# One hybrid decoder step on one core: expert programs written out instead of looped, the sample's dots read from PSUM, and 16 dots placed later

## The reference, cut to what matters

```python
def peer_ffn(h, wq, subkeys, u_tab, v_tab):            # h: normalised x, 1024 wide
    q = (xb @ wq).reshape(.., 8 heads, 2, 128)
    s = jnp.einsum('thpd,pkd->thpk', q, subkeys)        # two sets of 128 keys
    s1, i1 = lax.top_k(s[:, :, 0], 16); s2, i2 = lax.top_k(s[:, :, 1], 16)
    cand = s1[..., :, None] + s2[..., None, :]
    top_s, sel = lax.top_k(cand, 16)                    # 16 experts per head, of 16384
    g = jax.nn.softmax(top_s, axis=-1)
    u = u_tab[idx]
    act = jax.nn.gelu(jnp.einsum('thkd,td->thk', u, xb))
    vv = v_tab[idx]
    return jnp.einsum('thk,thkd->td', g * act, vv)
```

## Time and profile before

| | |
|---|---|
| runs of the kernel before | 2018.54, 2015.97, 2029.83 us (median 2018.54) |
| the profiled execution | 2016.57 us |
| its span | 2014.8 us |
| mean granted clock of TensorE, share of full speed | 0.903 |
| busy, share of the span | PE 78%, DVE 60%, POOL 56%, ACT 24% |
| DMA over the span | 713.45 MB, mean 354 GB/s |
| sample's mixer ends (last dot of tile 0) | 694.2 us |
| tiles 1 and 2 in the loops | about 960 to 1640 us |
| tile 3, straight | about 1640 to 1930 us |

### The profile page before, as it was taken

One profiled execution on the slowest core, in us unless ns is written; L12 is line 12 of the kernel. 1 busy time (PEld: TensorE's weight loads), 2 busy tenths in 40 slices (PEclk: granted clock), 3 DMA queues, 4 the chain that ended last, 5 costly groups with the idle time before them and its releaser, 6 DMA issues.

```text
span 2014.8 us, 20816 instructions
## 1 busy us (share of the span) xinstructions
PE 1579.8 (78%) x5461; PEld 746.2 (37%) x5461; DVE 1208.6 (60%) x3129; ACT 473.8 (24%) x1217; POOL 1122.4 (56%) x1168
## 2 busy tenths in 40 slices
PE   6989989987459358768788888698879789799943
PEld 1534546552127013214333344243334334354410
DVE  2223265869767602116667766667776579879973
ACT  1131313121001122212322222223232223332321
POOL 3000020223863545777777667667777767777774
PEclk9989999998775689998999989899999899999966
DMA  9796577798994799999999999999999999999997
GB/s 324 242 362 219 203 257 255 254 376 193 375 382 148 255 412 390 406 413 370 410 420 419 400 368 414 416 342 420 419 402 391 391 378 419 406 419 417 418 367 290
DMA packets 237576, 713.45 MB, mean 354 GB/s; under 512 B 23101, under 2 KB 49055, under 8 KB 237456
## 3 DMA queue, kind: packets, MB, share of 16 engines
q0 software_dynamic: 156672, 570.49, 72.4%
q1 hardware_dynamic: 80488, 140.73, 19.7%
q10 hardware_dynamic: 312, 1.07, 0.2%
HBM read 704.42 MB, written 8.25 MB: 354 GB/s over the span
## 4 chain that ended last, share of the span: by engine, by line
PE 18%; DMA 17%; DVE 10%; POOL 8%; issue 8%; ACT 3%; DVEq 0%; POOLq 0%; ACTq 0%
PE ps_y L2357 12%; DMA v_rows<-in_peer_v_dram,expert_idx_ring 7%; DMA v_rows<-in_peer_v_dram,tile_idx 6%; DVE u_rows L2136 5%; DMA u_rows<-in_peer_u_dram,expert_idx_ring 4%; PE ps_r L2331 4%; POOL u_rows L1916 3%; POOL v_rows L1922 3%; PE ps_y L2385 2%; POOL v_rows L1930 2%; ACT wt_diag L2027 1%; DVE key_scores_w L2147 1%; DVE top_i L2149 0%; DVE top L2148 0%; DVE top_i L2150 0%
## 5 line engine op out<-in xcount | busy, mean ns | idle before, releaser
L2357 PE MATMUL ps_y<-v_rows,wt_diag 128*128 128x512 f32 x1536 | 736.0, 620 | 140.3 <-DMA v_rows<-in_peer_v_dram,expert_idx_ring 75.1
L2357 PEld LDWEIGHTS ps_y<-v_rows,wt_diag 128*128 128x128 f32 x1536 | 285.7, 197 | 529.5 <-issue 515.6
L2136 DVE CUSTOM_DVE_ANT_0 u_rows<-u_rows,ps_y 128x1024 f32<-128x1024 f32 x360 | 420.6, 1217 | 70.5 <-DMA u_rows<-in_peer_u_dram,expert_idx_ring 64.4
L1916 POOL DMA_INDIRECT u_rows<-in_peer_u_dram,expert_idx_ring x384 | 369.6, 963 | 155.3 <-issue 92.3
L1922 POOL DMA_INDIRECT v_rows<-in_peer_v_dram,expert_idx_ring x384 | 365.2, 951 | 123.0 <-issue 99.6
L341 POOL DMA_INDIRECT low_rows<-in_peer_u_dram,tile_idx x128 | 165.6, 1294 | 210.3 <-DVE tile_dots L333 123.2
L608 PE MATMUL ps_z<-w_stream,hT 128*128 128x512 f32 (+5 forms) x560 | 245.9, 596 | 25.9 <-DVE hT L784 15.5
L2385 PE MATMUL ps_y<-v_rows,wt_diag 64*64 64x512 f32 x1024 | 134.7, 643 | 57.9 <-DMA v_rows<-in_peer_v_dram,tile_idx 53.7
L333 DVE CUSTOM_DVE_ANT_0 low_rows<-low_rows,tile_rows 128x1024 f32<-128x1024 f32 x128 | 153.2, 1230 | 40.6 <-DMA low_rows<-in_peer_u_dram,tile_idx 40.0
L1930 POOL DMA_INDIRECT v_rows<-in_peer_v_dram,tile_idx x128 | 121.4, 948 | 72.9 <-PE ps_y L2385 45.6
L608 PEld LDWEIGHTS ps_z<-w_stream,hT 128*128 128x128 f32 (+1 forms) x560 | 99.9, 183 | 150.5 <-issue 119.6
(11 more groups left out here) (442 smaller groups left out, 1691.7 us busy)
## 6 DMA issues: line engine op xcount, KB each, us to landing
w_stream<-in_w_in_dram SPq DMA_DIRECT2D x25, 2048.0 KB, 11.6
w_stream<-in_ada_w_dram SPq DMA_DIRECT2D x12, 2048.0 KB, 12.9
w_stream<-in_peer_wq_dram SPq DMA_DIRECT2D x8, 1024.0 KB, 8.3
wq<-in_peer_wq_dram SPq DMA_DIRECT2D x4, 2048.0 KB, 42.4
w_stream<-in_w_in_dram SPq DMA_DIRECT2D x5, 1568.0 KB, 9.6
w_stream<-in_w_in_dram SPq DMA_DIRECT2D x5, 1536.0 KB, 11.0
u_rows<-in_peer_u_dram,expert_idx_ring POOLq DMA_INDIRECT x384, 8.9
v_rows<-in_peer_v_dram,expert_idx_ring POOLq DMA_INDIRECT x384, 9.0
```

Source lines behind the costliest of these rows:

```text
L1916: g.indirect_dma_start(u_rows[:, j, :], None, U, bass.IndirectOffsetOnAxis(where[:, j:j + 1], 0))\
L2136: v.tensor_tensor_reduce(u_rows[:, j, :], u_rows[:, j, :], row[:, :], 1.0, 0.0, ALU.mult, ALU.add, dots[:, par, j:j + 1]).then_inc(s["u_us ...
L2357: mm = nc.tensor.matmul(ps_y[:, c * 512:(c + 1) * 512], diag[:, par, j, :], v_rows[:, j, c * 512:(c + 1) * 512], start=(first and j == 0), ...
```

## The change

1. The loops over t on POOL, ACT, DVE and PE, and the inner loops over pairs on ACT and PE, become Python loops: the programs of tiles 1 and 2 are written out, with constants for every wait and address.
2. A new method `row_to` copies `h0`, the dots' row, into two PSUM banks on DVE, and from there on the dots read it in PSUM. It is called three times: into `ps_n` in front of gap (3, "Z"), into `ps_z` in front of gap L, and into `ps_n` again in front of gap O. For this, OZ is copied out by ACT early (`act_oz`, right behind `act_front`), DVE waits for that before gap L and for `int_ready` before gap O, and PE waits for the dots up to gap L before it writes the attention scores into `ps_n`, and for the dots up to gap O before the output product goes into `ps_z`.
3. `DOTS_IN` has 3 dots instead of 6, 7 and 6 in the three gaps in front of the gates, and 16 more in gaps C to N. The gathers move with them.
4. Two semaphores of the constants become one; the waits stay where they were.

```diff
-           (3, "B"): 2, (3, "C"): 3, (3, "D"): 2, (3, "E"): 4, (3, "F"): 3, (3, "G"): 3, (3, "I"): 2, (3, "R"): 4, (3, "Z"): 6,
-           ("sample", "A"): 7, ("sample", "B"): 6, ("sample", "C"): 5, ("sample", "D"): 3, ("sample", "E"): 8,
-           ("sample", "F"): 5, ("sample", "G"): 5, ("sample", "K"): 6, ("sample", "L"): 9, ("sample", "N"): 12,
+           (3, "B"): 2, (3, "C"): 3, (3, "D"): 2, (3, "E"): 4, (3, "F"): 3, (3, "G"): 3, (3, "I"): 2, (3, "R"): 4, (3, "Z"): 3,
+           ("sample", "C"): 8, ("sample", "D"): 6, ("sample", "E"): 10, ("sample", "F"): 6, ("sample", "G"): 7,
+           ("sample", "K"): 8, ("sample", "L"): 11, ("sample", "N"): 13, ("sample", "O"): 12, ("sample", "Z"): 11}
...
-            self.nc.vector.tensor_tensor_reduce(self.rows[:, k % NB, :], self.rows[:, k % NB, :], self.X.h0[:, :], 1.0, 0.0,
+            self.nc.vector.tensor_tensor_reduce(self.rows[:, k % NB, :], self.rows[:, k % NB, :], self.row, 1.0, 0.0,
                                                 ALU.mult, ALU.add, self.keep["dots0"][:, k:k + 1]).then_inc(self.s["a_used"], 1)
+
+    def row_to(self, chain, banks):
+
+        self.row = banks[:, :, :].rearrange("p a n -> p (a n)")
+        chain(self.nc.vector.tensor_copy(self.row, self.X.h0[:, :]))
...
-        T.pool_og(pool)
+        T.pool_og(pool, oz_copied=True)
...
         T.act_front(act, chain)
+        T.act_oz(act)
...
         def behind_rows(eng):
 
+            eng.wait_ge(before["piece_out"], len(PIECES))
+            X.ahead.row_to(chain, X.ps_n01)
             left(eng)
             T.gap(eng, "A")
...
+        T.z_out(dve, OZ)
+        X.ahead.row_to(chain, X.ps_z01)
         T.gap(dve, "L")
...
+        dve.wait_ge(s["int_ready"], 1)
+        X.ahead.row_to(chain, X.ps_n01)
         T.gap(dve, "O")
...
         T.t_out(pe, S_K1)
+        pe.wait_ge(before["a_used"], DOTS_AT[("sample", "L")])
...
+        pe.wait_ge(before["a_used"], DOTS_AT[("sample", "O")])
         T.out_product(pe, lambda eng: T.on(eng, "oa_ready"), lambda eng: T.t_out(eng, S_HM))
...
-                with pool.Fori(0, LT - 1) as t:
+                for t in range(0, LT - 1):
                     for p in range(2, PPT + 2):
...
-                with act.Fori(0, LT - 1) as t:
-                    with act.Fori(1, PPT - 3) as p:
+                for t in range(0, LT - 1):
+                    for p in range(1, PPT - 3):
...
-                with dve.Fori(0, LT - 1) as t:
+                for t in range(0, LT - 1):
...
-                with pe.Fori(0, LT - 1) as t:
-                    with pe.Fori(1, PPT - 2) as p:
+                for t in range(0, LT - 1):
+                    for p in range(1, PPT - 2):
```

More of the change, by code:

```diff
@@ L114, in __init__ @@
         self.ident_ready, self.cleared, self.dist_ready = sem("const_ident"), sem("const_cleared"), sem("const_dist")
-        self.sdist_ready, self.s_step = sem("const_sdist"), sem("const_s_step")
+        self.s_step = sem("const_s_step")
         self.pool_ready = sem("const_pool")
@@ L129, in constants_dve @@
         v.memset(C.cols[h * NS:(h + 1) * NS, 1:2], -SLOPES[h])
-    dve.wait_ge(C.sdist_ready, 1)
+    dve.wait_ge(C.dist_ready, 1)
     v.tensor_tensor(C.tpat[:, :], C.tpat[:, :], K["ident"][:, :], ALU.mult).then_inc(C.s_step, 1)
@@ L139, in constants_dve @@
         .then_inc(C.s_step, 1)
-    dve.wait_ge(C.dist_ready, 1)
+    dve.wait_ge(C.dist_ready, 2)
     for h in range(AH):
@@ L192, in constants_pool @@
     g.tensor_copy(C.sdist[:, :], C.sdist_i[:, :])
-    g.tensor_copy(C.tpat[:, :], C.tpat_i[:, :]).then_inc(C.sdist_ready, 1)
+    g.tensor_copy(C.tpat[:, :], C.tpat_i[:, :]).then_inc(C.dist_ready, 1)
     g.tensor_copy(C.dist[:, :], C.dist_i[:, :]).then_inc(C.dist_ready, 1)
-    pool.wait_ge(C.dist_ready, 1)
+    pool.wait_ge(C.dist_ready, 2)
     for h in range(AH):
@@ L314, in __init__ @@
         self.rows = X.low[:, :].rearrange("p (j d) -> p j d", d=D)
+        self.row = X.h0[:, :]
         self.u_in = [nc.alloc_semaphore(f"mix_u0_in{j}") for j in range(NB)]
@@ L526, in __init__ @@
         self.ps_t, self.ps_m = ps("ps_t", [P, 4, P]), ps("ps_m", [P, 512])
-        self.ps_z = [ps("ps_z0", [P, 512]), ps("ps_z1", [P, 512])]
+        self.ps_z01 = ps("ps_z", [P, 2, 512])
+        self.ps_z = [self.ps_z01[:, 0, :], self.ps_z01[:, 1, :]]
         self.ps_s = ps("ps_s", [P, 2, 512])
-        self.ps_n = [ps("ps_n0", [P, 512]), ps("ps_n1", [P, 512])]
+        self.ps_n01 = ps("ps_n", [P, 2, 512])
+        self.ps_n = [self.ps_n01[:, 0, :], self.ps_n01[:, 1, :]]
         self.u = self.g7[:, 0:CW]
@@ L544 @@
            "o_full x1_ready x1_stored state_out pool_done act_step dve_step oz_ready").split()
-PROMPT_ONLY = "w_out_in init upd_full state_ready swa_full x1_stored state_out pool_done oz_ready inter_ready".split()
+PROMPT_ONLY = "w_out_in init upd_full state_ready swa_full x1_stored state_out pool_done inter_ready".split()
 ADA_SIGNALS = ("ada_c_in c_sgm c_silu ct_ps ct_ready picks bias_in gain_in part_full part_out row_full row_ready row_out0 row_out1 "
@@ L1587, in on_scalar @@
         a(intT, X.ps_n[1][:, 0:P], ACT.Copy).then_inc(s["int_ready"], 1)
-        T.act_norm(act, chain, X.ps_t[0:NS, :, :], lambda eng: T.t_landed(eng, S_I), "t_free")
+        T.act_norm(act, chain, X.ps_t[0:NS, :, :], lambda eng: T.t_landed(eng, S_I), "t_free", oz_copied=True)
         T.on(act, "pv_full")
```

## The result

Both kernels ran alternately on one chip: the changed kernel took 1991.4 us in the median (1986.5 to 1993.7, 4 runs), the kernel before 2019.5; the ratio is 0.985 with a 95% interval of 0.981 to 0.989, faster by 1.5%, 28 us. A second set, beside the experiments, gave 0.984 (0.980 to 0.988). The forecast was 1986, 31 us less, in the range of 1969 to 2006. Its profiled execution took 1993.35 us, with a span of 1991.6.

A forecast was written before the change was run, and what follows sets the result against it. The prediction took DMA, nearly matched by POOL's gather cadence, as the bound, with time lost where POOL waits for buffers. Mixer 13 plus experts 18 made 31 us off the profiled 2016.6, about 1986, range 1969 to 2006.

The forecast's parts named there:

- Mixer up to gap L: Sample's mixer front: gates ready before TensorE asks, its 21 us wait mostly hidden behind gathers; 39.4 MB at 392 GB/s, gain 4.4.
- the state C: Behind gap L: the load of C comes in early, so DVE's wait of 2.98 us goes; bounds 0 and 4.15.
- Gaps O and Z: Mixer's end: with the dots' row in PSUM gathers shorten, 29 to 31 plus copy 1.2 against 37.3 us; gain 6.
- The waits added to TensorE: Before attention scores and output product: two new waits for dots cost 0, up to 2.6 us if the first binds.
- The back edge: DVE's loop branch between tiles 1 and 2: the 9.43 us issue wait goes, with 9.9 us of POOL's lost time.
- the rest of the loops: Tiles 1 and 2: a quarter of POOL's remaining 32.5 us of waiting goes as DVE's loop register work disappears, 8 us.
- A: Whole kernel: the forecast itself, 1986 us, own range 1978 to 1995; chance 0.50.
- C: Mixer hardly gains: front bound by DMA, gathers stay slow despite the row in PSUM; 1996.6 us; chance 0.15.
- the rule cited for it: Trainium skill: DVE operations with two SBUF inputs leave descriptor generation alone, so gathers stay and gaps O and Z lose the copy.
- B: Experts: the loops come all the way to the straight tile's rate, 31 + 13 = 44 us, 1973; chance 0.13.
- D: Both gains half hidden, 5 us in the experts and 7 in the mixer, 2004.6; chance 0.15.
- E: Slower: fetches of straight programs exposed at 9.43 us each, 2038 us with 5 or 6 of them; chance 0.07.

The follow-up runs named there:

- again: The changed kernel unaltered, run a second time beside the experiments, against the kernel before: ratio 0.984 (0.980 to 0.988).
- mixer only: The changed kernel with its four loops put back, so only the mixer's part of the change, against the kernel before: ratio 0.992 (0.990 to 0.995).
- branches: The changed kernel with DVE's tile 2 in a loop of a single turn, same constants, against the kernel before: ratio 0.985 (0.983 to 0.987).
- 8 dots first: The changed kernel with 8 dots before gap (3, Z)'s routing, 5 taken from gaps E, K and L, against the kernel before: ratio 0.981 (0.978 to 0.985).
- the table of four: Old or new dot table with row in SBUF or PSUM; hT to v: old/SBUF 215.7, old/PSUM 210.5, new/SBUF 212.8, new/PSUM 206.4 us.

## Why the prediction was right, step by step

**The sum.** 13 + 18 = 31 was forecast; the ratios 0.985 and 0.984 of some 2020 us are 30 to 32, and the medians of the first set 28. The stages show 9.3 for the mixer (hT to v: 215.7 over the five profiles with the old mixer, 206.4 over the four with the new one) and 18.1 for the loops, 27.4 together. The loops' term was right, the mixer's 13 was too large by 4.

**Mixer up to gap L, 4.4 us, and the state C, 3.0.** The sum, 7.4, came out: from hT to C it is 126.6 us over the five profiles of the old mixer and 119.6 over the four of the new (changed, again, mixer only, branches), 7.0 less. The split was wrong, so that the match of the sum is partly luck. Gap L ends 116.0 us after hT in the mean before (112.5 to 118.7) and 115.5 after, 0.5 less; the other 6.5 lie behind it.

Two steps failed. The first is "bytes don't change in sum, only one row less has to land by the end of gap L": 0.5 MB less was forecast, and in the pair of profiles that is compared it was 0.16 MB less (42.69 to 42.53), over all profiles 0.4 MB more (42.1 to 42.5), since the loads of SyncE count too and the state C comes sooner. The second is the rate. The dip was there in each profile of the old mixer (252 to 314 GB/s in 10 us between 520 and 535) and is gone, but the whole stretch from hT to gap L's end went only from 362 to 366 GB/s, since the end of the stretch runs at 358 before and after; 392 had been taken for all of it. The kernel with the old table and the row in PSUM had no dip either (409 and 408 GB/s from 515 to 535) and still had C at 126.6.

That the 21 us wait of TensorE was mostly covered held. What it cost was the late load of C: issued 93.3 to 97.5 us after hT with the old mixer and 87.4 to 87.8 with the new, landed at 122.9 to 126.6 and 109.5 to 111.3. The moment of issue alone doesn't set it, for with 8 dots first it is 90.1 and C comes out no later (118.5).

**Gaps O and Z, 6 us.** In the two profiles they went from 37.3 to 32.6, the copy counted; over all profiles from 35.9 (34.2 to 37.9) to 32.5, 3.4 less. From C to the v rows it is 89.1 before and 86.8 after, only 2.3 less. The mechanism stands, and for the row's place alone 6 us were right (5 to 6 behind C, by the table of four). Two sizes were wrong: the first profile of before was among the long ones, and the thirteenth dot of gap N, taken to be free beside TensorE's matmuls, goes with 1.1 us more between C and gap O (49.0 to 50.1; 3 us where the table alone differs). These are the 4 us by which the mixer's sum was too large. A smaller one is the dot's 1.28 us from start to start, read from one pair: in gap Z of the changed kernel dots follow each other every 1.14 us.

**The waits added to TensorE, 0.** This held. No wait on the dots shows in the changed kernel's timeline in front of the attention scores or the output product.

**The back edge, 9.9, and the rest of the loops, 8.** Sum 18 forecast, 18.1 measured. The wait is gone, and POOL's surplus idle time fell from 42.4 to 16.5 us. The guess that TensorE's own loops cost nothing was borne out: DVE alone carries the gain. The split into 9.9 and 8 was not. In tile 1, where no back edge lies, straight code saves 333.4 - 326.3 = 7 us, in tile 2 344.4 - 333.5 = 11: so by this difference the back edge is worth some 4 us, and what the loop costs DVE besides some 14. The way from the candidate step to the first dot, 1.2 us a head shorter, would over sixteen heads be 19 us if DVE were always waited for, so it is large enough; no run takes out the register steps alone. The kernel with the mixer's part only agrees: its back edge is 5 us shorter, and its tile 2 no faster.

**The rivals.** The measured 1991.4 lies midway between A (1986) and C (1996.6), so the parts have to decide. B (1973) fell short: its condition came true, the tiles run at the 414 GB/s of the straight one, but that was worth 18 us and not 31; its estimate by the rates, 23, was nearer. C fell with the gathers at 0.94 us and 9 us in the mixer. By the prediction's own terms the rule cited for it would give 4.4 + 3.0 - 1.2 + 18 = 24, that is 1992 and not C's 1996.6, so the time alone would not have refuted it; the kernel with the row in SBUF refutes it. D fell with both parts. E never showed: no engine has a wait of that kind in the straight tiles.

## What to carry to other kernels

Where one engine's loop sits in front of the buffers that everything waits for, write out that engine's program first; here one of four carried the whole gain. When the DMA is full, count the bytes of every queue up to the mark, the loads of other engines too, before and after the change: here the gathers' row less was made up for by a load that came sooner. Work moved from in front of a late load to behind it isn't free there: the table's 7 us up to C came with 3 us behind it. Before a stage's difference of some microseconds is explained, read a second profile of the same kernel.

## What the runs showed that was not expected

- DVE's wait behind its loop's branch was 9.43 us in both profiles of one kernel, 9.39 in a second and 4.49 in a third, with the same body.
- The same gather instruction took up to 8.6 us beside dots with both operands in SBUF, and at most 0.97 when one of them is in PSUM, both from 495 to 600 us.
- Making gathers 0.28 us shorter in the median (1218 to 937 ns) gave the front up to the state C nothing: 58 gathers took the same 103 us, and with either table hT to C is the same for both places of the row.
- The start of the sample's part (hT) lay anywhere from 478 to 489 us in profiles whose program up to there is the same or nearly so.
